# One larger edit to a transformer block with retrieved experts: where the scores, the sixth adaptive vector and the first dense loads stand, and 144 instead of 128 tokens computed row by row

## What is computed

```python
n2 = rms_norm(h, g_norm2[l]) * (1 + scale2) + shift2
h = h + gate2 * peer(n2, w_pq[l], sub_keys[l], peer_u[l], peer_v[l])

def peer(xn, w_pq, sub_keys, u, v):
    q = (xf @ w_pq).reshape(t, PEER_HEADS, 2, PEER_HALF)
    sc = jnp.einsum("thpd,hpnd->thpn", q, sub_keys)
    vals, idx = lax.top_k(sc, PEER_TOPK)
    cand = (vals[:, :, 0, :, None] + vals[:, :, 1, None, :]).reshape(...)
    best, pos = lax.top_k(cand, PEER_TOPK)
    eidx = jnp.take_along_axis(cidx, pos, axis=-1)
    g = jax.nn.softmax(best, axis=-1)
    ...
    act = jax.nn.gelu(jnp.einsum("td,tkd->tk", xt, u[it])) * gt
    out = jnp.einsum("tk,tkd->td", act, v[it])
```

## Time and profile before

| what | us |
|---|---|
| median of 3 runs (lowest, highest) | 1687.42 (1686.39, 1690.63) |
| the profiled execution | 1689.35 |
| its span, first to last instruction | 1687.50 |
| PE busy | 1635.2 (97%) |
| DVE busy | 1376.5 (82%) |
| ACT busy, POOL busy | 584.1, 415.5 |
| mean granted clock of PE | 0.984 |

### The profile page before, as it was taken

How to read it: one execution, slowest core, us unless ns; L and a number is a source line. 1 busy time by engine, 2 the same in 40 slices (tenths; PEclk the granted TensorE clock), 3 DMA queues, 4 the chain that set the end, 5 groups by cost and what they waited for, 6 DMA issues and landing times. The chain is left out here.

```text
span 1687.5 us, 23884 instructions
## 1 busy us (share of the span) xinstructions
PE 1635.2 (97%) x7985; PEld 1360.0 (81%) x7985; DVE 1376.5 (82%) x2828; ACT 584.1 (35%) x824; POOL 415.5 (25%) x375
## 2 busy tenths in 40 slices
PE   6999999989999999999999999999999999999997
PEld 4877764755445999988989889898889898898986
DVE  6787857757998999977888787878888887888876
ACT  3335653232112666652222222322222222223223
POOL 0000000012553000003333333333335444444310
PEclk7999999989999999999999999999999999999999
DMA  9522125532221455579898979787898988899971
GB/s 376 187 102 75 57 112 168 189 125 66 91 69 50 150 194 206 188 268 317 326 322 289 324 271 319 277 315 290 288 321 313 327 299 315 309 337 349 330 250 50
DMA packets 138151, 388.51 MB, mean 230 GB/s; under 512 B 9440, under 2 KB 58720, under 8 KB 132064
## 3 DMA queue, kind: packets, MB, share of 16 engines
q1 hardware_dynamic: 100064, 251.27, 41.7%
q0 software_dynamic: 36864, 134.23, 21.9%
q10 hardware_dynamic: 1152, 2.10, 0.3%
HBM read 358.20 MB, written 29.36 MB: 230 GB/s over the span
## 5 line engine op out<-in xcount | busy, mean ns | idle before, releaser
L862 PE MATMUL ps<-Vs,As 128*128 128x512 f32 x2304 | 544.6, 392 | 3.6 <-DVE Vs L1650 3.6
L812 PE MATMUL ps<-xs,Us 128*128 128x384 f32 x2880 | 523.6, 336 | 0.3
L812 PEld LDWEIGHTS ps<-xs,Us 128*128 128x128 f32 x2880 | 503.2, 188 | 9.1 <-DVE Us L1605 1.1
L862 PEld LDWEIGHTS ps<-Vs,As 128*128 128x128 f32 x2304 | 432.9, 189 | 91.3 <-issue 4.3
L1162 ACT ACTIVATE att<-ps 128x384 f32<-128x384 f32 x96 | 47.3, 492 | 590.0 <-PE ps L812 590.0
L536 POOL DMA_INDIRECT big<-pv,islot x128 | 164.1, 1282 | 215.0 <-DVE low L1669 178.2
L536 POOL DMA_INDIRECT big<-pu,islot x128 | 144.3, 1127 | 221.1 <-DVE dot L1655 186.3
L1641 DVE TENSOR_TENSOR att<-att 128x384 f32<-128x384 f32 x96 | 53.4, 556 | 137.7 <-ACT att L1162 132.6
L590 PE MATMUL ps<-big 128*128 128x512 f32 (+1 forms) x384 | 157.0, 568 | 7.7 <-ACT big L904 5.6
L1669 DVE SCALAR_TENSOR_TENSOR low<-big,act_w,low 128x1024 f32<-128x1024 f32 x128 | 158.3, 1279 | 6.0 <-DMA big<-pv,islot 5.6
L1650 DVE TENSOR_TENSOR Vs<-big,Vs 128x1024 fp32r<-128x1024 f32 x128 | 156.0, 1219 | 0.0
(11 more groups left out here) (195 smaller groups left out, 1773.7 us busy)
## 6 DMA issues: line engine op xcount, KB each, us to landing
big<-puT SPq DMA_DIRECT2D x128, 512.0 KB, 4.7
big<-pv SPq DMA_DIRECT2D x64, 1024.0 KB, 9.1
big<-stream SPq DMA_DIRECT2D x31, 1024.0 KB, 5.3
gmat<-big SPq DMA_DIRECT2D x12, 2048.0 KB, 7.3
att<-gmat SPq DMA_DIRECT2D x31, 768.0 KB, 9.5
low<-wada SPq DMA_DIRECT2D x28, 512.0 KB, 4.7
work<-wada SPq DMA_DIRECT2D x12, 512.0 KB, 5.1
big<-wada SPq DMA_DIRECT2D x8, 512.0 KB, 13.5
```

Source lines behind the costliest of these rows:

```text
L812: mm = nc.tensor.matmul(ps[:, 6 + e, 0:DT], a, xs[:, b, k, :], start=(k == 0 and a is hi and b == 0), stop=(k == KT - 1 and a is lo))
L862: mm = nc.tensor.matmul(ps[:, 2 * b + half, :], a, Vs[:, e, w, half * T:(half + 1) * T], start=(opens and a is hi and w == 0), stop=(last ...
```

## The change

It does six things.

1. **Scores later.** PE's order is now: first tile of head w, scores of head w - 1, second tile of head w. The last scores stand behind the last tile.
2. **Sixth vector sooner.** `modulation(5)` stands behind `modulation(4)`, in a bank of its own, and DVE makes the norm's coefficients before the first multiply instead of before the third.
3. **16 more tokens by rows.** Tokens 128 to 143 get 16 extra slots: partition h*16 + t holds head h of token 128 + t. Their vectors are spread over the partitions by ACT (`nrep`) and 8 small fp32 products on PE, ACT copies them (`n_ext`); indices and weights get there by 16 small DMAs. So `u` and `v` are gathered and used 144 times each (NROWS), 2.48 rows a tile over tiles 2 to 59, 2.32 over tiles 60 to 121. Their sum is added over heads into the dense PSUM by two fp32 matmuls in the last turn.
4. **Fewer columns and groups.** Hidden tiles have 368 columns. The matrix is built in 92 groups (BUILT). Output tiles are unchanged.
5. **Nine gap tiles** (eight ahead of the lists), 23 early ones in the build, and 8 row buffers instead of 4.
6. **First routing slice sooner**: loaded ten groups before the build's end without its last two pieces, which ACT copies. DVE's dense part is written out instead of looped.

```diff
-ROWBUF = 4
+ROWBUF = 8
+XTOK = 16
+NROWS = XTOK + SLOTS
+UB = 60
+VE = 122
-GAP = 8
+GAP = 9
+SKIP = XTOK // 4
+BUILT = GROUPS - SKIP
...
+        u_row = [row[:, q, :] for q in range(4)] + [low[:, q * D:(q + 1) * D] for q in range(4)]
+        v_row = [row[:, q, :] for q in range(4)] + [big[:, (10 + q) * D:(11 + q) * D] for q in range(4)]
...
-            return (n - GAP) * GROUPS // (EARLY + 1 - GAP) + 1
+            return (n - GAP) * BUILT // (EARLY + 1 - GAP) + 1
...
+                if p == GROUPS - 10:
+                    for k in range(PRING):
+                        sp.wait_ge(piece_out[k], 16 * (PIECES // PRING - 1))
+                    sp.wait_ge(early_moved, 1)
+                    sp.dma_start(graw[:, 1, 0:PIECES - 2, :, :].rearrange("p h a t -> p h (a t)"),
+                                 gmat[0:PIECES - 2, :, 0:4 * HT].rearrange("h p f -> p h f")).then_inc(g_here[1], 16)
                 if p == GROUPS - 5:
                     sp.wait_ge(piece_out[0], 16 * (PIECES // PRING))
-                    sp.wait_ge(piece_out[1], 16 * (PIECES // PRING - 1))
-                    sp.wait_ge(early_moved, 1)
+                    sp.wait_ge(g_last, 1)
...
             modulation(4).then_inc(mod_done, 1)
+            modulation(5).then_inc(mod_done, 1)
...
+            for w in range(PH):
+                pq_tile(w, 0)
+                if w > 0:
+                    scores(w - 1)
+                pq_tile(w, 1)
...
+            scores(PH - 1)
...
-                        mm = nc.tensor.matmul(ps[:, 6 + e, 0:DT], a, xs[:, b, k, :],
+                        mm = nc.tensor.matmul(ps[:, 6 + e, XTOK:DT], a, xs[:, b, k, XTOK:DT],
...
+                if n == 2:
+                    pe.wait_ge(sc_ready, PH + 1)
+                    pe.wait_ge(spread_ready, 1)
+                    for k in range(KT):
+                        mm = nc.tensor.matmul(ps[:, 4 + k // 4, k % 4 * P:(k % 4 + 1) * P], nrep[:, k, :], ident[:, :],
+                                              start=True, stop=True)
+                    mm.then_inc(spread_done, 1)
...
+                    if last and d == 2:
+                        pe.wait_ge(row_used, NROWS + XTOK)
+                        for half in range(2):
+                            nc.tensor.matmul(ps[:, half, :], gath, acc_ext[:, half * T:(half + 1) * T],
+                                             start=False, stop=False)
...
             def second_coefficients(k):
-                if k == 2:
+                if k == 0:
...
+            def dot(r):
+                if r == 0:
+                    dve.wait_ge(ext_ready, 1)
+                row_wait(r)
+                v.tensor_tensor_reduce(out=u_row[r % ROWBUF], in0=u_row[r % ROWBUF],
+                                       in1=n_ext if r < XTOK else n_tok, scale=1.0, scalar=0.0,
+                                       op0=ALU.mult, op1=ALU.add, accum_out=dots[:, r:r + 1]).then_inc(row_used, 1)
...
+                    if 2 <= o < UB:
+                        for r in range(NROWS * (o - 2) // (UB - 2), NROWS * (o - 1) // (UB - 2)):
+                            dot(r)
+                    if o == UB:
+                        row_weights()
+                    if UB <= o < VE:
+                        for r in range(NROWS * (o - UB) // (VE - UB), NROWS * (o - UB + 1) // (VE - UB)):
+                            add_row(r)
```

More of the change, by code:

```diff
@@ L253, in build @@
         MOD3 = ps[:, 7, 0:MODS * KT]
+        MOD5 = ps[:, 5, 0:MODS * KT]
         def w_count(p):
@@ new lines, in pq_tile, with scores @@
+                pe.wait_ge(bank_free[n0 % BANKS], r * 2 + n0 // BANKS)
+                mm = product(ps[:, n0 % BANKS, :], lambda k: wring[:, p % 4, j, k, :], lambda k: nT[:, k, :],
+                             begins=j == 0, need=0 if w == j == 0 else None)
+                mm.then_inc(tile_done, 1)
+            def scores(w):
+                r, s = divmod(w, 4)
+                pe.wait_ge(bank_free[(N_PQ + 2 * s) % BANKS], r * 2 + (N_PQ + 2 * s) // BANKS + 1)
+                pe.wait_ge(bank_free[(N_PQ + 2 * s + 1) % BANKS], r * 2 + (N_PQ + 2 * s + 1) // BANKS + 1)
+                pe.wait_ge(sc_ready, w + 1)
+                if w == 0:
+                    pe.wait_ge(skw_here, 16)
+                for b in range(TB):
+                    for half in range(2):
+                        mm = nc.tensor.matmul(
+                            ps[:, 4 + b // 2, ((b % 2) * 2 + half) * NK:((b % 2) * 2 + half + 1) * NK],
+                            qh[:, s % 2, half, b * P:(b + 1) * P], skw[:, 2 * w + half, :], start=True, stop=True)
+                mm.then_inc(sc_done, 1)
+                transposed(2 + w, hT, w // 2, w % 2)
@@ new lines, in _ @@
+            for w in range(PH):
[3 more added lines that the diff above has]
+                pq_tile(w, 1)
+                if w == 0:
+                    pe.wait_ge(mod_ready, 5)
+                    for half in range(2):
+                        for q in range(4):
+                            mm = nc.tensor.matmul(ps[:, 6 + half, q * P:(q + 1) * P], ones[:, :],
+                                                  diag[:, 4 * half + q, :], start=True, stop=True)
+                        mm.then_inc(side_done, 1)
@@ L824, in _ @@
             pe.wait_ge(side_free, 2 * TB + 4)
+            for e in range(2):
+                nc.tensor.matmul(ps[:, 6 + e, 0:XTOK], zeros[:, :], ones[:, 0:XTOK], start=True, stop=True)
             for n in range(GAP - 1):
+                if n == 2:
[5 more added lines that the diff above has]
+                    mm.then_inc(spread_done, 1)
                 hidden_gap(n)
@@ L841, in _ @@
             nc.tensor.sem_inc(oh_used, 12)
-            for i in range(GROUPS):
+            for i in range(BUILT):
                 c = i % 4
@@ L1148, in deviation, with dense_turn @@
                 f(sstd[:, b:b + 1], ssum[:, b:b + 1], ACT.Sqrt, bias=eps[:, 0:1], scale=1.0 / D).then_inc(y_std, 1)
-            def dense_turn(g, last=False):
+            def dense_turn(g, last=False, weigh=False):
                 for d in range(BODY):
@@ L1202, in scale_rows @@
                         dve.wait_ge(gate_done, 2 * KT)
+                    if stage and between:
+                        between(k)
                     v.tensor_tensor(nT[:, k, :], hT[:, k, :], rstd, ALU.mult).then_inc(scaled, 1)
-                    if between:
+                    if between and not stage:
                         between(k)
@@ L1688, in norm @@
                                        ).then_inc(y_out, 1)
-            def dense_turn(g, rows, last=False, first=False):
+            for g in range(TURNS):
                 for d in range(BODY):
-                    nxt = d + 1
-                    if nxt % EVERY != EVERY - 1 and not (last and nxt == BODY):
+                    o, nxt = g * BODY + d, d + 1
+                    if nxt % EVERY != EVERY - 1 and o + 1 < XT:
                         i = nxt - nxt // EVERY
@@ L1734, in _ @@
+                    if o == XT - 2:
+                        norm(0)
             residual(1)
```

239 lines of the change are left out of this document (109 added, 130 removed).

## The result

The changed kernel takes 1665.47 us (median of five runs, 1662.88 to 1669.71) against 1687.27 beside it (1686.38 to 1690.63): a ratio of 0.9871, with a 95% interval of 0.9859 to 0.9882. That is 21.8 us or 1.3% less. The forecast was 1661.3, its range 1653 to 1679. The profiled execution took 1662.88 us, its span is 1661.0; the sum had said 1663.2 for it. So the sum over the one execution was right to 0.3 us, and the median lies 4.2 us above the forecast. Both facts need an explanation: the first because four terms of the sum were each off by more than 1 us and cancelled, which is luck, the second because the runs of the changed kernel spread over 7 us where those of the kernel before spread over 4.

A forecast was written before the change was run, and what follows sets the result against it. PE, busy 1635.2 of 1687.5 us, was taken as the bound. First group +1.8, build -11.5, opening -2.5, loop -15.6 and +1.7 gave -26.1 us: profiled 1663.2, median 1661.3, range 1653 to 1679.

The forecast's parts named there:

- Columns in build and dense loop: Hidden tiles of 368 instead of 384 columns save 0.163 us each: 3.7 us in 23 build tiles, 15.6 in 96 dense.
- The rival with a floor: Hidden matmuls: weight loads set a full floor under the pace, so narrower tiles give nothing; 1681 us, chance 0.06.
- the one with a third of the slope: Hidden matmuls: only a third of the column price holds, 12.9 us of the gain lost; 1674 us, chance 0.04.
- Scores, coefficients, gap tile: Second norm to first group: scores at 385.4, lists at 544.9, PE waiting about 4 us; first group 1.8 us later.
- I put 2.5 us on the ninth gap tile: Behind PE's wait for the lists: the clock drops and slows the ninth gap tile by 2.5 us.
- The build: Matrix build: four groups (3.5 us), one early tile (4.3) and columns (3.7) fewer, 11.5 us saved; bad end +2.
- margin of DVE: Build: DVE, 6.4 us short of full, loses 7.7 us of work against PE's 11.5; margin shrinks to about 2.6.
- The dense opening: Build's end to third hidden tile: slice wait goes, PE waits 2 to 3 us for U; -2.5 us, bounds -5 and 0.
- The dense loop: 96 hidden tiles save 15.6 us; gathering the 16 tokens costs two fp32 matmuls, +1.7 us.
- if not covered it is 3 us: Dense loop's head: four more gathers beside V buffers of tiles 4 to 7, taken as covered, otherwise 3 us.
- at most tenths of a us: Dense loop, tiles with three rows: 0.6 us of room between output tiles, at most tenths of a us lost.
- DVE becomes the bound: Dense loop: three-row tiles make one output tile in four 0.3 us late, 10 us; 1671 us, chance 0.08.

The follow-up runs named there:

- the experiment: For columns: changed kernel with hidden products over all 384 columns again, ratio 0.9974, median 1683.53 us. For the slice: first routing slice's load late again on the parted-gathers kernel, 0.9861.
- another kernel's: Changed kernel with scores directly behind their own pair's second tile again; ratio 0.9879, median 1669.3 us, profiled execution 1670.83 us.
- the quiet base: Changed kernel with parted gathers: rows 4 to 7 wait for tiles 4 and 5's V buffer, dot products begin at the fifth output tile; 1661.52 us, ratio 0.9842.
- slice late: Kernel with parted gathers, first routing slice's load behind the first V loads again; 1664.5 to 1665.1 us, ratio 0.9861.
- only the gate: Changed kernel with rows 4 to 7 waiting for tiles 4 and 5's V buffer, dot products still from the third output tile; 1664.51 us, ratio 0.9858.
- 384 columns: Changed kernel with hidden products over all 384 columns again, gap tiles too; median 1683.53 us, ratio 0.9974.

## Why the prediction was right, step by step

The direction and most of the size are right for the reason given, the columns. That the sum met the profiled execution to 0.3 us is luck: of its four stretches two gave more than forecast (by 3.4 and 2.7 us) and two less (by 1.3 and 4.4).

**Columns in build and dense loop (3.7 and 15.6): right.** 17.4 us by the experiment for these 19.3, 0.17 us a tile. The rival with a floor (0) and the one with a third of the slope (6.5) fell with it. The Trainium skill's sustained figures (TensorE: Matmul & The Clock Gate, Back-to-back issue gap) would have given a third. Its figure for an isolated matmul (columns at 2.4 GHz plus 2.5 ns) has the slope of these long streams, 0.417 ns a column; an estimate by it, 162.5 ns at 384 and 215.8 at 512, lies some 12 ns below the measured 174 and 228.

**Scores, coefficients, gap tile: mechanism right, the clock mis-sized.** Scores 384.48 for 385.4, lists 543.92 for 544.9, PE's wait 3.07 for about 4. The failing term is "I put 2.5 us on the ninth gap tile". In the profiled execution of the changed kernel it was 0. It is not zero for good: see the last section. The first group came 1.6 us sooner where the sum had 1.8 later: 3.4 us better, 2.5 by this term, 1.0 by the lists.

**The build: 10.2 for 11.5.** Up to 600 us an early tile with its four groups takes PE 7.57 us, as forecast (7.75 less 0.16 to 0.17); from there on it takes 7.65, and at the end PE waits twice for DVE's one-hot rows, 0.30 and 0.47 us, where it was once for 0.46. DVE is busy 173.15 of 177.81 us. So the margin of DVE that the prediction saw shrinking to 2.6 us was the right place to look for the waits at the end; what makes the 0.08 us a tile is not shown.

**The dense opening: 5.2 for 2.5.** The slice's wait went, and next in line was the U tile of the third hidden tile, as said; but PE waited 1.05 us for it and not 2 to 3, and the clock stayed. By the experiment, moving the slice is worth 3.2 us.

**The dense loop: 9.5 for 13.9.** This is the step that failed: "if not covered it is 3 us" for the eight gathers beside the V buffers was put down as covered, on the ground that PE would reach those tiles 30 us behind the build's end. Without the stop PE comes to tile 4 some 38 us behind it, and even that was too soon: the buffer was issued 16.4 us behind it and took 20.9, 37.3 in all, and ACT has to have it 2.5 us ahead of PE (765.51 and 767.97). It costs 2.0 us in the profiled execution, 3.3 plus 1.7 of half clock in another kernel's. With the gathers parted and the dot products later the median falls by 4.9, with the gathers alone parted by 1.9. The other part is the 16 rows: priced at 1.7 us for their matmul and "at most tenths of a us" for the tiles with three rows, they cost 3.9 us in the loop by the profile and 4.9 by the medians. The 2.2 us above the matmul are small stops of PE, the largest (0.47 us) behind a tile with three rows. With 2.0 for the stop that is 4.2 of the missing 4.4 us.

**What was not priced at all** is what eight row buffers earn. The prediction treated them as a cost; without them 144 rows cost all of the gain, 21 us. Whether four buffers would do for 128 rows in the shorter loop, or six for 144, was not run. The rival "DVE becomes the bound" had the right engine and asked only for its busy time, which was fine; the waits of the kernel with four buffers are for landings.

**Median.** 1661.3 was the sum less 1.9 us, the distance of the profiled execution from the median before. After, the median lies 2.6 above the profiled one. In the second measurement of the same kernel it was 4.0. The median of the kernel before came from three runs. A sum from one execution carries over to the median only if nothing in the change makes the runs spread.

## What to carry to other kernels

When buffers are added so that more transfers can be under way, look at the moment when all of them start at once, and at which load on another queue is due just then; hold the surplus back until that load is in. Price such buffers also by what they carry: a stream whose mean rate suffices can still stop an engine that has in-order work queued behind each item. And time that is freed ahead of a wait for another engine is worth nothing until more work is put there: here the later scores and the ninth gap tile pay together. Undone one at a time on the quiet base, they cost 3.7 and 6.8 us.

## What the hardware showed that was not expected

The same wait of PE left the clock alone in some executions and not in others. Behind the lists PE has waited 3.07 to 3.12 us in nine profiled executions of these kernels; in six of them the gap tile behind took 5.11 us, in three 6.8. The granted clock over 541 to 555 us, in the changed kernel, with parted gathers, and with the wait of 8.02 us (columns as above):

```profile
541.00:555.00 14.00, 10.79 (x58) 8.57 (x59) 12.91 (x34) 6.64 (x9) 0.00 (x0) 1.00 0.03 3
```

```profile
541.00:555.00 14.00, 11.06 (x50) 7.98 (x51) 12.91 (x34) 5.46 (x9) 0.00 (x0) 0.88 0.02 3
```

```profile
541.00:555.00 14.00, 10.68 (x43) 7.67 (x44) 11.93 (x31) 3.29 (x6) 0.00 (x0) 0.71 0.02 2
```

At the opening of the dense part a wait of 2.38 us left it alone (slice late), one of 2.05 us did not (only the gate: the 24 matmuls behind it took 5.84 us instead of 4.27). At the V buffer one of 2.86 us left it alone (384 columns: 4.33 us for the 18 matmuls behind it), one of 3.12 did not. So the length of the wait alone does not decide in this range, and a clock loss behind such a wait should stand in a sum as 0 or about 1.7 us, with a chance each (three in nine at the lists). What decides was not found.
